# Second mixer: decays of all four pairs of heads in a buffer each, diagonal blocks of three pairs copied by DMA, work reordered around both

## The reference

```python
proj = h @ w_in                     # q, k: 8 heads; v, z: 16 heads; of 128; and beta, a
qkv = silu(causal_conv(qkv))
q, k = l2norm(q), l2norm(k)
g = -exp(a_log) * softplus(a + dt_bias);  gc = cumsum(g)
decay = exp(where(lower, gc[:, None] - gc[None, :], -inf))
a_mat = where(strict, (k * beta) @ k.T * decay, 0)
t_mat = inverse(a_mat + eye)
u, w = t_mat @ (v * beta), t_mat @ (k * beta * exp(gc))
qk = where(lower, q @ k.T * decay, 0)
# scan over chunks: v_new = u - w @ S;  o = (q*exp(gc)) @ S + qk @ v_new;  S = S*exp(g_last) + k_dec.T @ v_new
o = rms_norm(o, norm_w) * silu(z)
y = o @ w_out
out = rms_norm(x + gate * y, final_g)
```

## Time and profile before

| | |
|---|---|
| median of three runs | 1099.07 us (1094.59 to 1099.57) |
| profiled execution, its own time | 1099.13 us |
| its span, first to last instruction | 1097.2 us |
| busy: TensorE, VectorE, ScalarE, GpSimd | 95%, 61%, 41%, 20% |
| mean granted TensorE clock | 0.981 |
| second mixer, first block of the convolution to the end | from about 529 us |
| z units and first half of heads, scan, second half, scan | 740, 826, 901, 972 us |

### The profile page before, as it was taken

How to read it: one execution, slowest core, us unless ns; L and a number is a source line. 1 busy time by engine, 2 the same in 40 slices (tenths; PEclk the granted TensorE clock), 3 DMA queues, 4 the chain that set the end, 5 groups by cost and what they waited for, 6 DMA issues and landing times. The chain is left out here.

```text
span 1097.2 us, 14427 instructions
## 1 busy us (share of the span) xinstructions
PE 1047.3 (95%) x5534; PEld 868.3 (79%) x5534; DVE 664.6 (61%) x1145; ACT 451.2 (41%) x838; POOL 215.8 (20%) x161
## 2 busy tenths in 40 slices
PE   9999999999999989999899999998999997989997
PEld 5888888888779878788778788787888876878886
DVE  4245435742056577766737757856695669866635
ACT  4223224342266563341533342458524458224432
POOL 0010000000000033103100001001105743135792
PEclk9999999999999989999899999999999998989999
DMA  8276624322052072142423445335322223203502
GB/s 302 79 261 223 223 89 147 112 95 96 0 194 59 1 247 85 58 137 75 163 77 115 159 149 204 143 136 190 110 82 80 90 82 96 77 20 107 183 1 77
DMA packets 60819, 132.35 MB, mean 121 GB/s; under 512 B 6097, under 2 KB 6481, under 8 KB 60625
## 3 DMA queue, kind: packets, MB, share of 16 engines
q1 hardware_dynamic: 58304, 118.67, 31.9%
q0 software_dynamic: 2304, 12.58, 3.2%
q10 hardware_dynamic: 144, 0.20, 0.0%
HBM read 117.22 MB, written 14.22 MB: 120 GB/s over the span
## 5 line engine op out<-in xcount | busy, mean ns | idle before, releaser
L292 DVE TENSOR_TENSOR w_lo<-raw,w_hi 128x2048 fp32r<-128x2048 f32 x58 | 133.9, 2309 | 206.5 <-ACT w_hi L288 198.9
L288 ACT ACTIVATE w_hi<-raw 128x2048 fp32r<-128x2048 f32 x51 | 97.5, 1913 | 206.1 <-PE projections_ps L131 138.3
L129 PE MATMUL projections_ps<-projections_x_hi,w_hi 128*128 128x512 f32 x208 | 81.1, 390 | 0.4 <-ACTq L513 0.4
L130 PE MATMUL projections_ps<-projections_x_lo,w_hi 128*128 128x512 f32 x208 | 80.9, 389 | 0.0
L131 PE MATMUL projections_ps<-projections_x_hi,w_lo 128*128 128x512 f32 x208 | 80.9, 389 | 0.0
L129 PE MATMUL projections_ps<-w_hi,projections_x_hi 128*128 128x512 f32 x192 | 74.7, 389 | 0.0
L130 PE MATMUL projections_ps<-w_lo,projections_x_hi 128*128 128x512 f32 x192 | 74.7, 389 | 0.0
L131 PE MATMUL projections_ps<-w_hi,projections_x_lo 128*128 128x512 f32 x192 | 74.7, 389 | 0.0
L249 DVE SCALAR_TENSOR_TENSOR resid<-resid,mixer_cw 128x512 f32<-128x512 f32 x96 | 66.6, 763 | 0.0
L2551 POOL TENSOR_TENSOR mixer_steps<-mixer_steps,mixer_logs 128x1024 f32<-128x1024 f32 x8 | 17.6, 2205 | 234.3 <-DMA mixer_steps<-logs_kept 234.3
L129 PE MATMUL mixer_ps<-w_hi,mixer_ha_hi 128*128 128x512 f32 (+1 forms) x132 | 53.7, 407 | 4.3 <-ACT tok L2299 3.9
(11 more groups left out here) (341 smaller groups left out, 2538.5 us busy)
## 6 DMA issues: line engine op xcount, KB each, us to landing
raw<-in_w_in SPq DMA_DIRECT2D x26, 1024.0 KB, 5.0
raw<-in_gdn_w_in SPq DMA_DIRECT2D x24, 1024.0 KB, 5.1
tok<-in_ada_w POOLq DMA_DIRECT2D x16, 768.0 KB, 6.3
raw<-in_w_out SPq DMA_DIRECT2D x8, 1024.0 KB, 6.5
qkv_kept<-mixer_ring SPq DMA_DIRECT2D x8, 1024.0 KB, 4.2
mixer_st<-qkv_kept SPq DMA_DIRECT2D x32, 256.0 KB, 2.9
raw<-in_gdn_w_out SPq DMA_DIRECT2D x8, 1024.0 KB, 5.7
resid<-in_att_bias SPq DMA_DIRECT2D x16, 256.0 KB, 2.7
```

The costliest lines, as they stand in the source:

```text
L129: nc.tensor.matmul(out, w_hi, x_hi, start=first, stop=False, skip_group_check=True)
L130: nc.tensor.matmul(out, w_hi, x_lo, start=False, stop=False, skip_group_check=True)
L288: self.nc.scalar.activation(self.hi[s][:], self.raw[s][:], ACT.Copy).then_inc(self.hi_ready, 1)
L292: engine.tensor_tensor(self.lo[s][:], self.raw[s][:], self.hi[s][:], ALU.subtract)\
```

## The change

- `steps` gets a buffer for each pair. The exponential is taken in place; `E` goes. The logs of the first half are loaded in the convolution's blocks 6 and 7 instead of in block 5 and among the pairs, all subtracted there, clipped ahead of the last block's taps, and the four exponentials are taken in `make_decays`. For the second half the logs are loaded together, GpSimd subtracts in the scan of pairs 0 to 2, VectorE clips in pairs 1 (n = 14), 2 (n = 6, 14) and 3 (n = 7), ScalarE takes two exponentials in pair 3 (n = 5, 13) and two between the squares.
- `compact` of pairs 0 to 2 becomes four DMAs of SP each, [32 partitions, 8 blocks, 32 values], counted by `cc_in`; pair 3 stays with ScalarE. The inverse waits for both.
- Banks: z units 4 and 5 get banks 4 and 5, y unit 2 and 3 too; the waits follow.
- Second half: m tiles 6 and 7 are turned before pair 2's build; y units 2 and 3 (their first halves) stand before and after pair 3's. Low halves of 6 and 7 are made behind pair 1. U of pair 0 is expanded by VectorE instead of GpSimd. The low halves of output tiles 2 and 3 are made in the inverse before steps 4 and 15; tile 3's was GpSimd's.
- The scratch area for GpSimd's DMAs shrinks from 8192 to 2048 bytes a partition.

The diff, cut:

```diff
-steps = sb("steps", [P, 2, 8, P])
+steps = sb("steps", [P, HB, 8, P])
...
-E = es[:, 1]
...
-Z_BANKS = (0, 1) * 4 + (6, 7, 2, 3, 4, 5, 0, 1)
-Y_BANKS = (1, 0, 6, 7, 2, 3, 0, 1)
+Z_BANKS = (0, 1, 0, 1, 4, 5, 0, 1, 6, 7, 2, 3, 4, 5, 0, 1)
+Y_BANKS = (1, 0, 4, 5, 2, 3, 0, 1)
...
-        if n >= 2:
-            sp.wait_ge(e_ok, n - 1)
+        if i:
+            sp.wait_ge(pt_ok, at(0, 1, j, 1))
-        sp.dma_start(flat(steps[:, j % 2]), a["logs2"][n].partition_broadcast(P)).then_inc(logs_in[j % 2], 16)
+        sp.dma_start(flat(steps[:, j]), a["logs2"][i * HB + j].partition_broadcast(P)).then_inc(logs_in[j], 16)
+
+    def compact(i, j):
+        sp.wait_ge(c_ok, at(i, 1, j, 1))
+        for r in range(4):
+            rows_r = slice(32 * r, 32 * r + 32)
+            sp.dma_start(Cc[rows_r, 8 * j:8 * j + 8, :], C[rows_r, 8 * j:8 * j + 8, rows_r]).then_inc(cc_in, 16)
...
             sp.wait_ge(spilled[0], 32)
             for j in range(2):
                 stage(0, j)
-                load_logs(0, j)
+        if n >= 7:
+            for j in range(2):
+                load_logs(0, 2 * (n - 7) + j)
     load(B_CONV + 1)
...
     stage(0, 2)
     load(B_CONV + 2)
-    load_logs(0, 2)
     sp.wait_ge(kk_made, at(0, 1, 1, 1))
+    compact(0, 0)
     stage(0, 3)
-    load_logs(0, 3)
     sp.wait_ge(kk_made, at(0, 1, 2, 1))
+    compact(0, 1)
     stage(0, 0)
     load(B_CONV + 3)
     sp.wait_ge(kk_made, at(0, 1, 3, 1))
+    compact(0, 2)
     stage(0, 1)
-    for j in range(2):
+    for j in range(HB):
         load_logs(1, j)
     sp.wait_ge(w.lo_ready, 2 * (B_CONV + B_Z) + 2)
...
     stage(1, 2)
-    load_logs(1, 2)
     sp.wait_ge(kk_made, at(1, 1, 1, 1))
+    compact(1, 0)
     stage(1, 3)
-    load_logs(1, 3)
     sp.wait_ge(kk_made, at(1, 1, 2, 1))
+    compact(1, 1)
     stage(1, 0)
+    sp.wait_ge(kk_made, at(1, 1, 3, 1))
+    compact(1, 2)
+    stage(1, 1)
     sp.wait_ge(wo_lo[0], 2)
     load_out(4)
-    sp.wait_ge(kk_made, at(1, 1, 3, 1))
-    stage(1, 1)
     sp.wait_ge(wo_lo[1], 2)
     stage_v(1, 0)
...
-                if 2 <= u < 8 or u >= 14:
-
-                    pe.wait_ge(zp_out, u - 1 if u < 8 else u - 7)
+                if 2 <= u < 4:
+                    pe.wait_ge(zp_out, u - 1)
+                elif 6 <= u < 8:
+                    pe.wait_ge(zp_out, u - 3)
+                elif u >= 12:
+                    pe.wait_ge(zp_out, u - 7)
...
-                pe.wait_ge(sq_ok, at(1, 8, HB - 1, 8))
-                pe.wait_ge(tok_out, at(1, 1, HB - 1, 1))
+                pe.wait_ge(m_lo_ok, 8)
...
             build(1, 0)
             y_unit(1, 0)
             build(1, 1)
-            build(1, 2)
-
             turn_m(6, 4)
             turn_m(7, 5)
+            build(1, 2)
+            y_unit(2, 0)
             build(1, 3)
+            y_unit(3, 0)
             y_pair(0, 1)
-            y_pair(2, 0)
             y_pair(2, 1)
...
+    def exps(i, j):
+        act.wait_ge(clipped, at(i, 1, j, 1))
+        nc.scalar.activation(steps[:, j], steps[:, j], ACT.Exp, scale=-1.0).then_inc(e_ok, 1)
+
+        for j in range(HB):
+            exps(0, j)
...
-    def exps(i, j):
-        act.wait_ge(clipped, at(i, 1, j, 1))
-        if j:
-            act.wait_ge(c_ok, at(i, 1, j - 1, 1))
-            act.wait_ge(pt_ok, at(i, 1, j - 1, 1))
-        nc.scalar.activation(E, steps[:, j % 2], ACT.Exp, scale=-1.0).then_inc(e_ok, 1)
-
...
     squares(0, 0)
-    exps(0, 0)
     round_z(1, 0)
     evacuate_z(2)
     evacuate_z(3)
     round_z(1, 1)
     squares(0, 1)
-    compact(0, 0)
-    exps(0, 1)
     squares(0, 2)
-    compact(0, 1)
-    exps(0, 2)
     evacuate_z(4)
     evacuate_z(5)
     round_z(2, 0)
     squares(0, 3)
-    compact(0, 2)
-    exps(0, 3)
     round_z(2, 1)
     compact(0, 3)
...
             act.wait_ge(heads_out, i)
             squares(1, 0)
-
-            act.wait_ge(z_gated, HB)
-            exps(1, 0)
             squares(1, 1)
-            compact(1, 0)
-            exps(1, 1)
-            squares(1, 2)
-            compact(1, 1)
             exps(1, 2)
             for e in (6, 7):
                 high(e, e - 2)
+            squares(1, 2)
+            exps(1, 3)
             squares(1, 3)
-            compact(1, 2)
-            exps(1, 3)
             compact(1, 3)
+            round_out(2, yp_half, 1)
             evacuate_y(0)
             evacuate_y(1)
-            round_out(2, yp_half, 1)
             evacuate_y(2)
             evacuate_y(3)
...
+                elif i == 0 and n in (5, 13):
+                    exps(1, n // 13)
...
-        pool.wait_ge(logs_in[j % 2], 16 * (i * 2 + j // 2 + 1))
+        pool.wait_ge(logs_in[j], 16 * (i + 1))
-        rows = steps[:, j % 2].rearrange("p (h c) l -> p h c l", h=2)
+        rows = steps[:, j].rearrange("p (h c) l -> p h c l", h=2)
...
     clear_semaphores(pool, ended)
-    for j in range(2):
+    for j in range(HB):
         log_decay_steps(0, j)
     begin(0)
     for i in range(NB):
-        for j in range(2, HB):
-            log_decay_steps(i, j)
         pool.wait_ge(kss_ok, at(i, 1, HB - 1, 1))
         nc.gpsimd.tensor_tensor(flat(rinv[:]), flat(kss[:]), half[:, 0, :], ALU.pow).then_inc(rinv_ok, 1)
-        if i:
-            out_rest(nc.gpsimd, pool, 3)
-        pool.wait_ge(uc_ok, i * 2 + 1)
+        pool.wait_ge(uc_ok, i * 2 + 2)
         pool.wait_ge(pt_ok, at(i, 1, HB - 1, 1))
-        expand(i, 0, Uc, U[0], ux_ok)
-        pool.wait_ge(uc_ok, i * 2 + 2)
+        pool.wait_ge(ux_ok, at(i, 2, 0, 2))
         expand(i, 1, Tc, T, tx_ok)
         expand(i, 1, Uc, U[1], ux_ok)
         out_rest(nc.gpsimd, pool, 4 * i)
-        if i == 0:
-            for j in range(2):
-                log_decay_steps(1, j)
         for j in range(HB):
             if j:
...
+            if i == 0 and j + 1 < HB:
+                for n in ((0, 1), (2,), (3,))[j]:
+                    log_decay_steps(1, n)
...
+    def clip(i, j):
+        dve.wait_ge(steps_ok, at(i, 1, j, 1))
+        nc.vector.tensor_scalar(steps[:, j], steps[:, j], 0.0, None, ALU.max).then_inc(clipped, 1)
+
+        if b == B_CONV - 1:
+            for j in range(HB):
+                clip(0, j)
...
-
-    def clip(i, j):
-        dve.wait_ge(steps_ok, at(i, 1, j, 1))
-        nc.vector.tensor_scalar(steps[:, j % 2], steps[:, j % 2], 0.0, None, ALU.max).then_inc(clipped, 1)
...
-        if j and j + 1 < HB:
-            clip(i, j + 1)
-        E_j = E.rearrange("p (h c) e -> p h c e", h=2)
+        E_j = steps[:, j].rearrange("p (h c) e -> p h c e", h=2)
...
-        dve.wait_ge(cc_ok, at(i, 4, HB - 1, 4))
+        dve.wait_ge(cc_in, 16 * 4 * (HB - 1) * (i + 1))
+        dve.wait_ge(cc_ok, 4 * (i + 1))
...
+        dve.wait_ge(pt_ok, at(i, 1, HB - 1, 1))
+        for grp in range(2):
+            expand_group(nc.vector, 0, grp, Uc, U[0], ux_ok)
...
-        if i == 0:
-            for j in range(2):
-                clip(0, j)
-            if i and j == 2:
+            if i and j == 1:
-            invert_32(i, {9: lambda: out_rest(nc.vector, dve, 2)})
+            invert_32(i, {4: lambda: out_rest(nc.vector, dve, 2), 15: lambda: out_rest(nc.vector, dve, 3)})
...
+                    elif i == 0 and (j, n) in ((1, 14), (2, 6), (2, 14)):
+                        clip(1, j - 1 + n // 14 * (j - 1))
-                elif i == 0 and n in (7, 9):
-                    clip(1, n // 9)
+                elif i == 0 and n == 7:
+                    clip(1, 3)
...
```

More of the change, by code:

```diff
@@ L1612, in second_mixer @@
         logs_made, logs_out, logs_kept = (sem(n) for n in ("logs_made", "logs_out", "logs_kept"))
-        logs_in = [sem(f"logs_in{i}") for i in range(2)]
+        logs_in = [sem(f"logs_in{i}") for i in range(HB)]
         steps_ok = sem("steps_ok")
@@ L1618, in second_mixer @@
         pt_ok = sem("pt_ok")
-        cc_ok = sem("cc_ok")
+        cc_ok, cc_in = sem("cc_ok"), sem("cc_in")
         kss_ok = sem("kss_ok")
@@ L1726, in load_logs @@
             def load_logs(i, j):
-                n = i * HB + j
-                if n >= 2:
-                    sp.wait_ge(e_ok, n - 1)
+                if i:
+                    sp.wait_ge(pt_ok, at(0, 1, j, 1))
                 else:
                     sp.wait_ge(logs_kept, 16 * TT)
-                sp.dma_start(flat(steps[:, j % 2]), a["logs2"][n].partition_broadcast(P)).then_inc(logs_in[j % 2], 16)
+                sp.dma_start(flat(steps[:, j]), a["logs2"][i * HB + j].partition_broadcast(P)).then_inc(logs_in[j], 16)
[4 more added lines that the diff above has]
+                    sp.dma_start(Cc[rows_r, 8 * j:8 * j + 8, :], C[rows_r, 8 * j:8 * j + 8, rows_r]).then_inc(cc_in, 16)
             def load_out(v):
@@ L2963 @@
     from concourse.bass_utils import run_bass_kernel_spmd as _run
-    nc = _bacc.Bacc("TRN2", target_bir_lowering=False, num_devices=1, dynamic_dma_scratch_size=8192)
+    nc = _bacc.Bacc("TRN2", target_bir_lowering=False, num_devices=1, dynamic_dma_scratch_size=2048)
```

## The result

The changed kernel takes 1108.27 us (median of 4 runs, 1107.46 to 1108.44); the kernel before, on the same chip, 1098.67 (4 runs, 1094.59 to 1099.57). The ratio is 1.0097, 95% interval 1.0079 to 1.0114: slower by about 1%, where no change was forecast (1098.7), and above the range. The profiled execution took 1108.22 us; its span is 1106.4, 9.2 more than before.

The account below looks back on a forecast made before the run. TensorE, busy 95% of the span, was taken as the bound: only its waits or clock could move the time. First half +4.0, first scan +1.5, second half -5.8 sum to -0.3: 1098.7 us, own range 1095.5 to 1102.

Parts of the forecast that it names:

- The convolution, +3.5: Convolution (650 to 740 us): clips ahead of the last taps start unit 3 later by 2.6 to 4.6 us, taken as 3.5.
- the bound of 4.6: Convolution: upper end of the later start of unit 3, with 2.6 us of clips and subtractions holding them 2 us.
- what the early 1.79 gives back is swallowed: Convolution: removing TensorE's earlier 1.79 us wait gains nothing, since TensorE only comes sooner to z unit 1's evacuation wait.
- The z units, -6.0 + 4.75 + 1.7: First half, 740 to 826 us: 6.0 us of waits and clock loss go; a new 4.75 us wait and 1.7 of clock come.
- The wait for unit 6: First half's z units: TensorE's 3.9 us wait goes, as unit 6 no longer shares its bank with unit 4.
- The first scan, +1.5: First scan (826 to 901 us): three clips moved among chunks where GpSimd works, at 0 to 2 us each, taken as 1.5.
- unit 12's wait: First half: TensorE waits 4.75 us at z unit 12, as the inverse waits for pair 2's copies; 1.7 of clock added.
- The bound of 4: First scan: upper bound of the clips' cost, bounds 0 and 4 us, with only one clip in a tight place.
- The second half, -5.8: Second half (901 to 972 us): inverse begins 2.2 us sooner, is 3.5 shorter, 0.1 for an expansion; bounds -3.5 and -7.5.
- the copies that don't stand behind the load: Rival, first half: copies land in 2 us, TensorE waits 2.2, the clock may stay; 1092.3 us in all; chance 0.25.
- the slower one: Rival, both halves: copies land like the 9.4 us load, delaying both inverses; +9.7, 1108.8 us in all; chance 0.18.
- The third rival, the port: Rival, convolution and scan: clips and GpSimd's subtractions meet each time, convolution 4.6, scan 4; 1102.3 us in all; chance 0.08.

Follow-up runs that it names:

- e3: e1 with all four loads of the first half's decays issued one convolution block earlier: 1094.9 us (ratio to the kernel before 0.9965).
- e1: The changed kernel with three of VectorE's clips in the first scan moved later, one of them out of pair 2, chunk 1: 1097.3 us (ratio to before 0.9996).
- e9: The changed kernel with GpSimd's subtraction for pair 2 of the next half moved from behind pair 1 to behind pair 2, clips unmoved: 1098.4 us (ratio to before 1.0003).
- e2: e1 with pair 2's four copies of the first half issued before the load of the last weight tile: 1092.4 us (ratio to the kernel before 0.9944).
- e5: The kernel before with three added clips, without effect on values, on VectorE in pair 2, chunk 1 of the first scan: 1105.4 us (ratio 1.0059).
- e10: The kernel before with two added clips where e5 had three, in pair 2, chunk 1 of the first scan: 1097.6 us (ratio 0.9998).

## Why the prediction was wrong

The forecast was -0.3; its terms, in order:

- **The convolution, +3.5; measured +4.7**, just above the bound of 4.6. The working was right in kind, clips behind the last two subtractions. Two things in it were wrong and offset each other. The hold, put at 0 to 2 us in all, was 4.3 (6.89 less 2.6), as subtractions and memset came one behind the other. And "what the early 1.79 gives back is swallowed" was not so: VectorE's low half ahead of the clips starts 72.17 us into the stretch, where the kernel before has 74.25, and 2.6 + 4.3 - 2.1 is 4.8. e3 shows it from the other side, where the stall is back. TensorE's wait came in one piece of 4.7 and not in two, with windows at 0.94 and 0.89 behind it that the forecast hadn't priced either. That the exponentials cost nothing was right: behind the table load Silu still waited 1.09 us for the taps.
- **The z units, -6.0 + 4.75 + 1.7; measured 0.0 for 0.45.** The steps were right, and that the sum met is in part luck. The wait for unit 6 went; VectorE stood 5.77 us ahead of its transpose (6.6 forecast), the copies' issue took 2.55 us for four in place of 1.6, their landing 2.7 (793.63 less 790.92) in place of 4.5, whose 1.5 us for the short pieces no row had shown, and TensorE waited 4.15 (4.75). The clock behind it fell to 0.83 in one window, 1.7 us as forecast; in e1 and e9, with the same code there, it was 3.4 us (0.77 and 0.89) behind 4.3 of wait. The order of the queue made the stall, not the price of short pieces; e2 shows it.
- **The first scan, +1.5; measured +10.1. This is the step that failed.** The prediction named the place ("the one in pair 2, chunk 1 stands ahead of an addition that the next chunk needs") and the range of one held operation, 0 to 2 us; the clip's extra was 1.9 and TensorE's wait 2.14, so that size was right to within 0.2. What was left out is the clock. The 1.7 us counted behind unit 12's wait was not counted here, and here it was 8.6: 17 us at half clock behind 2.1 us of wait. e5 gets it in the kernel before, e1 and e9 take it away. The bound of 4 was worked out from VectorE's rows alone, and no row of a wait in a scan was at hand to price its clock.
- **The second half, -5.8; measured -6.2.** Right: it began 1.8 us sooner (2.2), and was 4.4 shorter (3.5). Of the difference of 0.9 in length 0.6 is that the expansions of T run beside an idle GpSimd, 1.29 us for two where the earlier trace rows has 1.89. TensorE's wait grew to 5.7; the prediction had "about 7 then". The -0.9 behind it is the clock of one execution: behind a wait of 5.66 us the changed kernel lost 1.7 us (0.83), and e1, e2 and e9, with the same code and 5.67, lost 3.4.

Of the rivals, the copies that don't stand behind the load were half right (landing 2.7) and wrong in the outcome; the slower one gave 1108.8, which is the measured time, for a reason that didn't happen: no row shows a landing near 9.4, and the second inverse waited for no DMA. A number that agrees is no evidence. The third rival, the port, is the one that ran, in both places. It had 0.08 and a price of 4 in the scan, as it too priced the hold and not the clock behind it. The Trainium skill (SBUF — State Buffer, the reading of the diagram) states that the first of the two engines keeps the shared ports for its whole instruction; by that rule, the trace agrees: the clip that came 0.30 us late was held to the product's end, and the second one of the convolution waited out a memset, which reads nothing, as well. Not every operation of GpSimd holds: one on 128x8 values, 2.12 us long in e5 and 2.20 in e10, ran beside the added clips, and they took 2.04 for three and 1.29 for two, as long as alone. (The trace's spans of GpSimd are rough, so this is a sign, not a proof.)

What isn't settled is why waits of 4 to 5 us in the z units cost 1.7 to 3.4 us of clock, while 1.73 and 2.14 in the scan cost 6.9 and 8.6, nor why one and the same wait costs 1.7 in one execution and 3.4 in another. All were measured; no run here tells what the differences are made of.

## What to carry to other kernels

Price a wait of the bounding engine with its clock: look up what earlier waits of that engine cost in the windows behind them, and where a stretch shows no such wait, take as an upper bound a long stay at half clock (17 us here), not the wait's own length. Before putting a small operation of VectorE into a tight place, look at what GpSimd will run at that moment under the new order, not the old; adding work to GpSimd moves its long products onto other operations. And an engine's DMA must not stand in a queue behind a load that waits for the same engine.

## What the runs showed of the hardware that was not expected

- A wait of 0.97 us of TensorE in the scan cost no clock (e10), one of 1.73 us 6.9 us (e5), one of 2.14 us 8.6 (the changed kernel): nearer to a step than to a slope, by one profiled execution of each.
- TensorE stayed at half clock through a window in which it was busy 10.00 of 10 us (890 to 900), and came back only near 902.
- A DMA with short pieces cost its queue more: 0.61 us in the median (2.55 for four) where the stagings of q and k took 0.43 and the loads of decays 0.50. Its landing took 2.4 us in the median and 4.7 at most over 24, where the earlier trace rows had 3.8 and 9.4 for loads of such pieces.
